# Decay exponential that takes in beta, and scan steps in another order, in a two-layer hybrid state-space and MoE kernel

## What is computed

```python
# SSD:     y = (C B^T * decay) x  +  exp(acs) * (C h)          h = exp(acs_end) h + B^T (decay_end x)
# HGRN2:   o = (q k^T * w) v      +  (q exp(b)) s              s = exp(b_last) s + (k exp(b_last - b))^T v
# gated DeltaNet:
decay = exp(gam_t - gam_s)                       # t >= s, else 0
a_strict = strict((k * beta) @ k.T * decay)      # beta per token and head
sol = triangular_solve(a_strict + I, rhs)        # unit lower triangular
qk = (q @ k.T) * decay
# out_ssd = y + d_skip * x, both directions summed
```

## Time and profile before

| | |
|---|---|
| median of 3 runs | 2721.14 us (2718.81 to 2727.26) |
| the profiled execution | 2721.68 us, its span 2720.0 us |
| busy shares | PE 88%, DVE 43%, ACT 24%, POOL 23% |
| mean granted TensorE clock | 0.932 |

### The profile page before, as it was taken

One profiled execution on the slowest core, in us unless ns is written; L12 is line 12 of the kernel. 1 busy time (PEld: TensorE's weight loads), 2 busy tenths in 40 slices (PEclk: granted clock), 3 DMA queues, 4 the chain that ended last, 5 costly groups with the idle time before them and its releaser, 6 DMA issues.

```text
span 2720.0 us, 44348 instructions
## 1 busy us (share of the span) xinstructions
PE 2392.9 (88%) x14316; PEld 1570.8 (58%) x14317; DVE 1177.7 (43%) x2831; ACT 660.7 (24%) x1223; POOL 622.5 (23%) x740
## 2 busy tenths in 40 slices
PE   4999788888889999999996798778887999999996
PEld 2446677777645555555554345667775555555553
DVE  4542367666423333333333443356643333333333
ACT  2116443432301111111111214534312111111111
POOL 1000255550002222222221000126510222222221
PEclk9999888888989999999998899888888999999998
DMA  6652300002629999999996352200036999999994
GB/s 256 236 192 62 51 1 1 1 1 79 238 97 367 360 355 349 338 350 342 367 344 188 139 183 69 52 1 1 1 130 223 351 366 375 376 356 355 378 358 153
DMA packets 187950, 574.19 MB, mean 211 GB/s; under 512 B 55774, under 2 KB 99110, under 8 KB 148902
## 3 DMA queue, kind: packets, MB, share of 16 engines
q1 hardware_dynamic: 162982, 520.48, 51.6%
q0 software_dynamic: 24832, 51.97, 8.2%
HBM read 554.89 MB, written 53.15 MB: 224 GB/s over the span
## 4 chain that ended last, share of the span: by engine, by line
PE 62%; DMA 12%; DVE 12%; issue 5%; ACT 4%; POOLq 2%; DVEq 1%; SPq 1%; ACTq 1%; POOL 0%
PE ps L1894 56%; DMA featT<-ffn_rows,idx_in 8%; PE ps L1898 5%; DVE R L1240 4%; ACT R L917 3%; DMA R<-ffn_rows,idx_in 3%; DMA R<-in_exp_up 1%; POOLq L829 1%; DVE R L1519 1%; DVE featT L1240 1%; DVE R L1243 1%; DVE h L1240 1%; DVE ring L1240 1%; ACTq L914 1%; DVEq L1237 1%
## 5 line engine op out<-in xcount | busy, mean ns | idle before, releaser
L1894 PE MATMUL ps<-R 128*64 128x256 f32 (+7 forms) x8872 | 1417.3, 389 | 70.5 <-DVE R L1240 18.3
L1894 PEld LDWEIGHTS ps<-R 128*64 128x64 f32 (+3 forms) x8872 | 864.5, 167 | 492.8 <-issue 259.4
L917 ACT ACTIVATE R<-ps 128x256 f32<-128x256 f32 (+3 forms) x343 | 156.1, 455 | 978.1 <-PE ps L1894 853.5
L1894 PE MATMUL ps<-featT,ring 128*128 128x512 f32 (+1 forms) x768 | 316.4, 569 | 0.3 <-issue 0.3
L1240 DVE TENSOR_TENSOR R<-R,ps 128x256 f32<-128x256 f32 (+2 forms) x208 | 122.2, 588 | 435.3 <-ACT R L917 369.3
L1894 PEld LDWEIGHTS ps<-featT,ring 128*128 128x128 f32 x768 | 148.8, 198 | 163.3 <-issue 158.2
L1243 DVE TENSOR_SCALAR R<-ps,idx_out 128x512 f32<-128x512 f32 x128 | 96.1, 750 | 273.6 <-PE ps L1894 273.6
L1249 DVE COPY R<-ps 128x512 f32<-128x512 f32 (+2 forms) x280 | 153.7, 549 | 127.4 <-PE ps L1898 99.6
L853 POOL DMA_INDIRECT ffn_sum_even<-R,idx_out x64 | 94.8, 1481 | 479.3 <-DVE idx_in L1240 361.7
L853 POOL DMA_INDIRECT ffn_sum_odd<-R,idx_out x64 | 103.7, 1621 | 436.1 <-issue 285.6
L917 ACT ACTIVATE R<-ps,idx_out 128x512 f32<-128x512 f32 x128 | 88.0, 688 | 384.1 <-PE ps L1894 384.1
(11 more groups left out here) (218 smaller groups left out, 1964.6 us busy)
## 6 DMA issues: line engine op xcount, KB each, us to landing
R<-in_exp_gate SPq DMA_DIRECT2D x128, 1024.0 KB, 9.6
R<-in_exp_up SPq DMA_DIRECT2D x128, 1024.0 KB, 18.0
R<-in_exp_down SPq DMA_DIRECT2D x128, 1024.0 KB, 16.6
R<-in_w_mod SPq DMA_DIRECT2D x48, 1024.0 KB, 7.1
ring<-in_w_in SPq DMA_DIRECT2D x30, 1024.0 KB, 5.3
ring<-in_w_out SPq DMA_DIRECT2D x4, 1024.0 KB, 6.7
R<-in_w_out SPq DMA_DIRECT2D x4, 1024.0 KB, 6.4
ffn_sum_odd<-zero SPq DMA_DIRECT2D x6, 512.0 KB, 9.1
```

Of the source, the lines that this page charges most:

```text
L917: do(C.activation(out_, in_, func, **kw), name)
L1894: return MM(out_, lhsT, rhs, start=start, stop=stop)
```

## The change

Eight edits, all in the scans of both layers. (1) `beta` is held at 1e-37 or more by DVE and replaced by its logarithm (ACT, once a layer); `e_gdn` is four 128x128 exponentials with that logarithm as bias in place of one 128x512, and `keyed` is one 128x512 product in place of four 128x128 with beta. For that, the two halves of `key_products` change banks. (2) `hdec`, the end column of `eb`, is copied by ACT behind `eb` in place of DVE, in two buffers. (3) `e_gdn(u+1)` stands behind the first `Pm` copies. (4) `own_quarters` stands behind the first half of the SSD steps. (5) `hgrn_scans(u+1)` stands ahead of `w_next(u, 0)`. (6) `ssd_out` loses its last one or two steps, which become `ssd_sum`, done a unit later ahead of `w_next`. (7) In `own_steps` the product goes to PSUM (`less`, bank 0), and the start value is no longer copied in each unit. (8) `h_levels(u, 1)` on DVE and `h_products(u, 1)` on PE stand ahead of `ssd_out` and `ssd_outputs`.

```diff
-        hdec = sb("hdec", [P, 2])
+        hdec = sb("hdec", [P, 2, 2])
...
-        dv = cut(HH, BLK)
-        dt8 = cut(HH, BLK)
+        dv = cut(2, HH, BLK)
...
                 def e_gdn(u):
                     wait("pre_ps", 3 * u + 1, l)
-                    f(Eg[u % 3][:, :, :].rearrange("p h t -> p (h t)"), ps[:, 6, :], ACT.Exp, "e_gdn")
+                    _, d, c = UNITS[u]
+                    for q in range(HH):
+                        ins = C.activation(Eg[u % 3][:, q, :], ps[:, 6, tk(q)], ACT.Exp, bias=beta[:, c, d, q:q + 1])
+                    do(ins, "e_gdn")
...
+                f(beta[:, :, :, :], beta[:, :, :, :], ACT.Ln)
...
-                    f(eb[:, :], bh[:, :], ACT.Exp, "eb_ready")
-                    if u + 1 < U:
-                        e_gdn(u + 1)
+                    f(eb[:, :], bh[:, :], ACT.Exp)
+                    end = P - 1 if d == 0 else 0
+                    f(hdec[:, u % 2, :], eb[:, :].rearrange("p (t s) -> p t s", t=2)[:, :, end], ACT.Identity, "eb_ready")
                     for a in range(MID):
                         for hf in range(2):
                             half_copy(u * NP + 2 * a + hf + 3, hf, Pm)
                         if a == 0:
+                            if u + 1 < U:
+                                e_gdn(u + 1)
                             if u + 2 < U:
                                 steps(Mg, u + 2, range(HS, NDEC))
                             act.drain().then_inc(S["m_ready"], 1)
                         if a == 1:
+                            if wanted:
+                                do(steps(Ms, u, range(HS // 2)))
                             if u + 1 < U:
                                 own_quarters(u + 1)
-                            if wanted:
-                                do(steps(Ms, u, range(HS // 2)))
...
+                ts(beta[:, :, :, :], beta[:, :, :, :], 1e-37, None, ALU.max)
...
                 def keyed(u, out_, at_):
 
-                    _, d, c = UNITS[u]
-                    for q in (0, 2, 1, 3):
-                        V.scalar_tensor_tensor(out_[:, q, :], ps[:, 7 - q % 2, at_ + (q // 2) * P:at_ + (q // 2 + 1) * P],
-                                               beta[:, c, d, q:q + 1], Eg[u % 3][:, q, :], ALU.mult, ALU.mult)
+                    pairs = lambda v: v.rearrange("p (a b) t -> p a b t", a=2)
+                    V.tensor_tensor(pairs(out_), ps[:, 6:8, at_:at_ + 2 * P].rearrange("p b (a t) -> p a b t", a=2), pairs(Eg[u % 3][:, :, :]), ALU.mult)
...
-                        cp(dv[:, :, :], unit8[:, :].unsqueeze(1).to_broadcast([P, HH, BLK]))
                         wait("pre_ps", 3 * u + 3, l)
                     rep = ps[:, 1, 2 * P:4 * P].rearrange("p (q t r) -> p q t r", q=HH, t=BLK)
+                    now, less = dv[:, d, :, :], ps[:, 0, 0:HH * BLK].rearrange("p (q t) -> p q t", q=HH)
                     for n in range(first, last):
                         r, to = (n, slice(n + 1, BLK)) if d == 0 else (BLK - 1 - n, slice(0, BLK - 1 - n))
-                        tt(dt8[:, :, to], rep[:, :, to, r], dv[:, :, r:r + 1].to_broadcast([P, HH, BLK - 1 - n]), ALU.mult)
-                        tt(dv[:, :, to], dv[:, :, to], dt8[:, :, to], ALU.subtract)
+                        old = now if n else unit8[:, :].unsqueeze(1).to_broadcast([P, HH, BLK])
+                        tt(less[:, :, to], rep[:, :, to, r], now[:, :, r:r + 1].to_broadcast([P, HH, BLK - 1 - n]), ALU.mult)
+                        tt(now[:, :, to], old[:, :, to], less[:, :, to], ALU.subtract)
...
                     if SEEN[c] == u:
                         tt(yraw[:, c, 0:SW], tmp[:, :], ps[:, 7, :], ALU.add, "ssd_sb")
-                        tt(by_head(tmp[:, :]), xs(c), heads(dsk[:, :]), ALU.mult)
                     else:
                         tt(tmp[:, :], tmp[:, :], ps[:, 7, :], ALU.add, "ssd_sb")
-                    tt(yraw[:, c, 0:SW], yraw[:, c, 0:SW], tmp[:, :], ALU.add)
+
+                def ssd_sum(u):
+                    _, d, c = UNITS[u]
+                    if c in live:
+                        if SEEN[c] == u:
+                            tt(by_head(tmp[:, :]), xs(c), heads(dsk[:, :]), ALU.mult)
+                        tt(yraw[:, c, 0:SW], yraw[:, c, 0:SW], tmp[:, :], ALU.add)
...
+                for d in range(2):
+                    cp(dv[:, d, :, :], unit8[:, :].unsqueeze(1).to_broadcast([P, HH, BLK]))
...
                     dve.drain().then_inc(S["kend_ready"], 1)
+                    if more_:
+                        hgrn_scans(u + 1)
+                    if u > 1:
+                        ssd_sum(u - 2)
                     w_next(u, 0)
                     if u:
                         gdn_end(u - 1)
                     if more_:
-                        hgrn_scans(u + 1)
                         keys(u + 1)
                         queries(u + 1)
                     w_next(u, 1)
...
                     w_next(u, 2)
+                    if wanted:
+                        h_levels(u, 1)
                     if u:
                         ssd_out(u - 1)
-                    if wanted:
-                        h_levels(u, 1)
                     if more_:
...
+                ssd_sum(U - 2)
...
+                ssd_sum(U - 1)
...
-                            ins = mm(ps[:, 7 - par, tk(a + 10 - x)], cv[rows, 10 + a, tk(c)], cv[rows, x + a, tk(c)])
+                            ins = mm(ps[:, 6 + par, tk(a + 10 - x)], cv[rows, 10 + a, tk(c)], cv[rows, x + a, tk(c)])
...
-                key_products(0, 0)
+                key_products(0, 1)
                 wait("e_gdn", 1, l)
-                key_products(0, 1).then_inc(S["pre_ps"], 1)
+                key_products(0, 0).then_inc(S["pre_ps"], 1)
...
                         if a == 2:
+                            if wanted:
+                                wait("h_cp", (un - 1) * 4 + 1, l)
+                                h_products(u, 1)
                             if u:
                                 ssd_outputs(u - 1)
                             if more_:
                                 repeats(u + 1)
-                            if wanted:
-                                wait("h_cp", (un - 1) * 4 + 1, l)
-                                h_products(u, 1)
```

More of the change, by code:

```diff
@@ L1471, in keys @@
                     wait("pre_ps", 3 * u + 2, l)
-                    keyed(u, AT[u % 2], 0)
+                    keyed(u, AT[u % 2][:, :, :], 0)
                     dve.drain().then_inc(S["at_ready"], 1)
@@ L1499, in own_put @@
                         wait("vn_ps", u - 1, l)
-                    tt(W[u % 2][:, 1, :, :].rearrange("p q (b t) -> p q b t", t=BLK), dv[:, :, :].unsqueeze(2).to_broadcast([P, HH, P // BLK, BLK]),
+                    tt(W[u % 2][:, 1, :, :].rearrange("p q (b t) -> p q b t", t=BLK), dv[:, UNITS[u][1], :, :].unsqueeze(2).to_broadcast([P, HH, P // BLK, BLK]),
                        blk[:, :].rearrange("p (b t) -> p b t", t=BLK).unsqueeze(1).to_broadcast([P, HH, P // BLK, BLK]), ALU.mult, "t_ready")
@@ L1547, in hgrn_state @@
                         wait("hs_ps", u + 1, l)
-                        add_blocks(Sh[:, d, :, :], hdec[:, :], ps[:, 5, 2 * P:4 * P])
+                        add_blocks(Sh[:, d, :, :], hdec[:, u % 2, :], ps[:, 5, 2 * P:4 * P])
                     dve.drain().then_inc(S["hgrn_done"], 1)
@@ L1619, in _ @@
                     wanted, more_ = c in live, u + 1 < U
-                    end = P - 1 if d == 0 else 0
                     if u:
@@ L1627, in _ @@
                     wait("eb_ready", u + 1, l)
-                    cp(hdec[:, :], eb[:, :].rearrange("p (t s) -> p t s", t=2)[:, :, end])
                     if wanted:
```

## The result

The changed kernel takes **2649.28 us** (median of 4 runs, 2648.27 to 2655.68), the kernel before 2720.26 on the same chip: a ratio of **0.9739**, with 95% within 0.9716 to 0.9762, or 71 us less. The forecast was 2689 us with a range from 2657 to 2706, so it was wrong: the gain is twice as large as forecast. The profiled execution took 2648.36 us, its span is 2646.7 us and its mean granted clock 0.950, in place of 0.932.

The account below looks back on a forecast made before the run. The prediction took a chain of waits through PE, DVE and ACT as the bound, DVE holding about 15 of 37 us per unit. Savings in both layers less 3.4 us for starts gave 32.6 us, so 2689 us, range 2657 to 2706.

Parts of the forecast that it names:

- I take every wanted unit to have this once.: Assumption that each wanted unit has one low-clock fall over the long PE stretch, 6.8 us at the lower level.
- TensorE's clock stays up: Rival: with less waiting ahead of PE's long stretch the clock holds, 26 us more gain, 2663 us; chance 0.22.
- two waits go: Argument for the clock staying up: PE's waits for DVE ahead of `ssd_outputs` and `h_products(2)` go; no size of its own.
- The first DVE stretch, 0.7: DVE from `w_next` to `scores`: `ssd_outputs` on PE starts earlier, 0.7 us saved per unit, bounds 0.2 and 1.75.
- The second DVE stretch, 1.3: From `ssd_outputs` to `h_products(2)`: `h_levels(1)` no longer behind `ssd_out`, 1.3 us saved, 2.3 where `ssd_out` had four steps.
- that covers it: Claim that the later `ssd_out` (1.5 us) delays nothing, since its reader `ssd_new_state` stands behind `h_products(2)`.
- No gain on the path: Terms for `hdec`, `e_gdn`, `own_quarters` and, in wanted units, `own_steps`: each counted as 0 us.
- in wanted units this lies beside ACT's 6.6 us: 0: Claim that faster `own_steps` differences save 0 in wanted units, being beside ACT's work at the unit's end.
- Unwanted units, 2.0 each: Units 0 to 3 of layer 1: 1.0 us from the first DVE work and 1.0 from `own_steps`, 2.0 saved each.
- The start, 1.7 lost per layer: Start of each layer's scans: `Ln` of beta, its table load and longer `e_gdn(0)`, less shorter `keys(0)`, lose 1.7 us.
- It ends slower: Rival: PE's clock falls a second time in each wanted unit, 3.4 us x 12 = 41, so 2730 us; chance 0.05.
- PE or ACT took a part of the gain: Rival: smaller first-stretch and unwanted-unit gains and later `ssd_new_state`, 2703 us likely, 2709 at worst; chance 0.18.

Follow-up runs that it names:

- fill2: Kernel before with two spare 128x128 products behind the first 64x64 group and two ahead of `h_products(2)`, in ten wanted units: 2704.76 us, ratio 0.9939.
- b8: Kernel before with only `h_levels(u, 1)` moved ahead of `ssd_out` and `h_products(u, 1)` ahead of `ssd_outputs`: 2704.08 us, ratio 0.9953 to the kernel before.
- a_no7: Changed kernel with the `own_steps` product back out of PSUM and the start copy restored: 2675.52 us, ratio 0.9831 to the kernel before.
- a_late: Changed kernel with two idle DVE steps, about 1.5 us, ahead of `scores` in ten wanted units: 2697.41 us, ratio 0.9930 to the kernel before.

## Why the prediction was wrong

**The step that failed: "I take every wanted unit to have this once."** The forecast kept the stretch of low clock of the earlier trace rows in each wanted unit, and gave *TensorE's clock stays up* a chance of 0.22. It stayed up: 1.00 from `repeats(2)` to `repeats(7)` of layer 0, and 95 us less low clock in both layers' scans. By an estimate from the measured prices, 0.26 to 0.37 us each, that is 25 to 35 us of the 68.2; the remaining 33 to 43 stand against the 32.6 forecast as direct. The rival's mechanism was right. That its 26 us are right too is in part luck: it took 2.2 us in each of 12 units, where unit 3 shows 1.75 and `fill2` 1.96, and 82 us of low clock (12 times 6.8) where 95 went, not all of it from wanted units. One of these, in layer 1, still fell. Its argument "two waits go" agrees with all runs. What spoke against it, that the 64-row products and the wait for ACT stay, was not enough: both stayed, and the clock held, though `fill2` shows that waits there do count. The Trainium skill's "TensorE: Matmul & The Clock Gate" (What's actually happening) says that activity releases a throttle which is there by default; `fill2`, where nothing but spare products was added, agrees, 0.88 to 1.00 over those five intervals. The same page's "A second HAM failure mode: psum-queue depth-cycling" tells of another kernel in which frequent short idle times between groups of matmuls let the clock swing between its two levels. Unit 3 of before agrees in this: the clock fell behind waits of 0.16 to 1.30 us.

**The first DVE stretch, 0.7.** Right: 0.60, and the room of 1.61 us was filled, with DVE just ahead of PE's demand. `ssd_sum`'s two steps took 0.85 each in place of 0.69, with POOL busy beside them, without harm.

**The second DVE stretch, 1.3.** Right: 1.35. `h_products(2)` starts 2.2 us behind the end of `ssd_outputs`, as said. But "that covers it", said of the later `ssd_out`, looked at `ssd_new_state` alone. `own_steps` and `h_levels(2)` stand behind it too, and `b8` shows what that costs without edits 6 and 7.

**No gain on the path.** `e_gdn` in four steps and in its new place delayed nothing in unit 3, where the long stretch has no gap. For `own_steps` "in wanted units this lies beside ACT's 6.6 us: 0" was wrong, in a second and smaller step: only steps 3 to 6 lie there. The first three and the start copy stand ahead of `h_levels(2)`, for which PE waits, and taking edit 7 back made the waits for `h_levels` 7.3 us longer in all.

**Unwanted units, 2.0 each.** The wait for `own_put` fell from 3.95 to 2.94 us behind `repeats(2)` and `repeats(3)`, and from the 4.38 of the earlier trace rows to 3.24 behind `repeats(4)`: the 1.0 that was forecast. It is edit 7's, for `a_no7` has 3.94, 3.94 and 4.38 there. From `repeats(1)` to `repeats(5)` of layer 1 the four intervals together are 11.4 us shorter, 94.8 in place of 106.2:

```profile
1722.10:1816.90 94.80, 78.98 (x595) 69.87 (x593) 58.93 (x179) 43.04 (x118) 44.27 (x65) 0.89 0.01 1
```

```profile
1763.90:1870.10 106.20, 81.42 (x579) 72.70 (x578) 67.54 (x205) 39.96 (x102) 44.65 (x66) 0.86 0.00 1
```

The first is the changed kernel, the second before. The low clock is 21 us against 30, some 3 us of the 11.4; the rest is about the 8 that were forecast.

**The start, 1.7 lost per layer.** Right. ACT's timeline at the start of layer 0:

```profile
309.13 1.28 ACT L916 ACT_TABLE_LOAD   x1
310.43 0.23 ACT L916 ACTIVATE R<-R 128x32 f32<-128x32 f32 x1
310.73 1.27 ACT L1066 ACTIVATE ring<-past_,R 128x128 f32<-128x128 f32 x4
312.07 1.28 ACT L1073 ACT_TABLE_LOAD   x1
314.23 1.14 ACT L1073 ACTIVATE X<-ps,R 128x128 f32<-128x128 f32 x4 [0.88 <-PE ps L1909]
```

The second load starts at 312.07 where the only one of the earlier trace rows started at 310.36, 1.71 us later, and the first `repeats` start at 325.6 in place of 324.0. No drain shows ahead of either load.

**The other rivals.** *It ends slower* named the clock too, with the other sign; `a_late` shows that this side was real, for one delay of 1.5 us in a unit brings it back. No sign that PE or ACT took a part of the gain shows in unit 3. (In that rival's sum the last 3 us have no stated source; nothing else hangs on it.)

## What to carry to other kernels

Where the granted clock is below 1.00 in a latency-bound loop, price it first: it can double a gain, as here, or triple the cost of a delay, as in `a_late`. So give it more than a side case's chance when the change closes waits of TensorE. It pays only where no other wait takes the place of the low clock, as `b8` shows. A few spare products among the small products where it falls, as in `fill2`, show in one run what it is worth before anything is rearranged. And read what stands ahead of a step on its own engine up to the next thing that another engine waits for, not only what runs beside it: that is how edit 7 came to be worth something, and edit 8 alone so little.

## What was not expected of the hardware

- The longest wait of a stretch need not be the one that lowers the clock. With 1.30 us filled, the clock still fell in most units; with it left and waits of 0.47 and 0.24 us between small products filled, it stayed at 1.00 from `repeats(2)` to `repeats(7)`.
- A 1.5 us delay cost 1.5 us with the clock up and 5.2 us (15.7 over three intervals) with the fall that it brought.
- A difference of `own_steps` with one input in PSUM takes 0.16 to 0.18 us in every unit looked at, where the form with both in SBUF took up to 0.83 and, in unit 2 of `b8`, 1.27. The rule of the Trainium skill's "GPSIMD Engine Reference" (Specifications), weighed in the prediction, holds here.
